# Three of eight row pairs by seven products in the gate-and-up loop, with one weight sum of each on GpSimd

## The reference, cut to what matters

```python
D_MODEL, SEQ = 2048, 256
D_FF = ((8 * D_MODEL // 3 + 255) // 256) * 256      # 5632

def swiglu(x, w_gu, w_down):
    g, u = jnp.split(x @ w_gu, 2, axis=-1)
    return (jax.nn.silu(g) * u) @ w_down

h = h + 0.5 * rmsnorm(swiglu(rmsnorm(h, n_ffn1_pre), w_ffn1_gu, w_ffn1_down), n_ffn1_post)
...
h = h + 0.5 * rmsnorm(swiglu(rmsnorm(h, n_ffn2_pre), w_ffn2_gu, w_ffn2_down), n_ffn2_post)
```

## Time and profile before

| what | value |
|---|---|
| median of three executions | 2454.83 us |
| the profiled execution: time | 2453.54 us |
| the profiled execution: span | 2451.7 us |
| TensorE busy, weight load busy | 2434.3 us, 2019.7 us |
| VectorE busy, ScalarE busy, GpSimd busy | 1662.5 us, 1290.2 us, 439.6 us |
| chunks 1 to 10 of the first layer, of the second | about 57.6 to 479.2 us, 1782.2 to 2203.8 us |

### The profile page before, as it was taken

One profiled execution on the slowest core, in us unless ns is written; L12 is line 12 of the kernel. 1 busy time (PEld: TensorE's weight loads), 2 busy tenths in 40 slices (PEclk: granted clock), 3 DMA queues, 4 the chain that ended last, 5 costly groups with the idle time before them and its releaser, 6 DMA issues.

```text
span 2451.7 us, 31974 instructions
## 1 busy us (share of the span) xinstructions
PE 2434.3 (99%) x11047; PEld 2019.7 (82%) x11047; DVE 1662.5 (68%) x2077; ACT 1290.2 (53%) x1556; POOL 439.6 (18%) x867
## 2 busy tenths in 40 slices
PE   9999999999999999999999999999999999999998
PEld 7888888888888888888888888888888888888887
DVE  6888888855556456677676564465688888885444
ACT  6555555544445456657575444444655555554442
POOL 5212112232012103223142020010112121211000
PEclk9999999999999999999999999999999999999999
DMA  7777777677678765555665676766677677767664
GB/s 242 215 209 215 209 207 220 206 237 217 201 223 263 203 185 161 172 160 160 166 185 164 196 210 194 229 217 191 213 207 221 200 219 206 215 210 252 195 192 145
DMA packets 306061, 498.50 MB, mean 203 GB/s; under 512 B 28461, under 2 KB 102321, under 8 KB 305201
## 3 DMA queue, kind: packets, MB, share of 16 engines
q1 hardware_dynamic: 282336, 457.85, 62.9%
q0 software_dynamic: 23344, 38.95, 5.1%
q10 hardware_dynamic: 288, 0.52, 0.1%
HBM read 471.39 MB, written 8.52 MB: 196 GB/s over the span
## 4 chain that ended last, share of the span: by engine, by line
PE 95%; POOL 1%; DVE 1%; DMA 1%; SPq 1%; issue 1%; ACT 0%; DVEq 0%; POOLq 0%; ACTq 0%
PE acc L727 56%; PE acc L815 30%; PE mix L815 4%; POOL mkh L690 1%; PE acc L770 1%; DMA sq<-mk_scratch 1%; PE acc L752 1%; POOL mkh L687 1%; SPq L396 0%; PE mix L788 0%; SPq L429 0%; PE mix L997 0%; DMA raw<-w_ffn_gu 0%; PE mix L1043 0%; PE mix L1077 0%
## 5 line engine op out<-in xcount | busy, mean ns | idle before, releaser
L1204 ACT ACTIVATE whi<-raw 128x1024 fp32r<-128x1024 f32 x860 | 910.4, 1060 | 1089.7 <-PE acc L727 685.6
L1701 DVE TENSOR_TENSOR wlo<-raw,whi 128x1024 fp32r<-128x1024 f32 x860 | 1044.1, 1225 | 607.5 <-ACT whi L1204 598.5
L815 PE MATMUL acc<-whi,x_lo 128*128 128x512 f32 x1000 | 389.0, 389 | 0.0
L815 PE MATMUL acc<-whi,x_hi 128*128 128x512 f32 x1000 | 389.0, 389 | 0.0
L815 PE MATMUL acc<-wlo,x_hi 128*128 128x512 f32 x1000 | 389.0, 389 | 0.0
L727 PE MATMUL acc<-whi,u_hi 128*128 128x512 f32 x896 | 356.9, 398 | 0.0
L345 POOL DMA_DIRECT2D nat<-nat x416 | 203.4, 497 | 823.9 <-DVE nat L1911 656.7
L727 PE MATMUL acc<-whi,u_lo 128*128 128x512 f32 x896 | 349.4, 390 | 0.0
L727 PE MATMUL acc<-wlo,u_hi 128*128 128x512 f32 x896 | 349.1, 390 | 0.0
L727 PE MATMUL acc<-wlo,act_hi 128*128 128x512 f32 x688 | 267.7, 389 | 0.0
L727 PE MATMUL acc<-whi,act_hi 128*128 128x512 f32 x688 | 267.7, 389 | 0.0
(11 more groups left out here) (423 smaller groups left out, 2928.1 us busy)
## 6 DMA issues: line engine op xcount, KB each, us to landing
raw<-w_ffn_gu SPq DMA_DIRECT2D x352, 512.0 KB
raw<-w_ffn_down SPq DMA_DIRECT2D x176, 512.0 KB
raw<-w_in SPq DMA_DIRECT2D x224, 256.0 KB
raw<-w_in SPq DMA_DIRECT2D x96, 512.0 KB
raw<-w_mem_kv SPq DMA_DIRECT2D x32, 512.0 KB
raw<-w_out SPq DMA_DIRECT2D x32, 512.0 KB
nat<-nat POOLq DMA_DIRECT2D x416, 32.0 KB, 3.9
raw<-w_in SPq DMA_DIRECT2D x64, 128.0 KB
```

The costliest lines, as they stand in the source:

```text
L815: ins = nc.tensor.matmul(bank, sides[a], weights[b], start=start and m == 0, stop=stop and m == 2)
L1204: act(whi[:, l % RING], raw[:, l], ACT.Copy).then_inc(hi_ready, 1)
L1701: tt(wlo[:, l], raw[:, l], whi[:, l % RING].bitcast(fp32), ALU.subtract).then_inc(lo_ready, 1)
```

## The change

`SEVEN_AT` becomes (2, 4, 6): three pairs of eight by seven products. The in-place sum of the up unit goes to GpSimd (`right_sum`); it waits for the second of VectorE's sums, since that one reads what it overwrites. In GpSimd's queue the sum for the first seven stands ahead of the 16 DMAs of the swap, the other two behind them. ScalarE's upper part of the up unit waits for GpSimd's semaphore. VectorE makes the lower parts of the two units of an eight in one operation (`split_pair`), in the odd slot; those of a seven stay single. The combining operations move from slots 12 and 13 to slots 14 and 15. The activation sums of the third seven get room: the side tensors lie elsewhere, `a_sum` in the place of `wsum`, and their split in chunk 0 is made in three pieces one slot later.

```diff
@@ -86,7 +86,7 @@
 SKEW = RING
 QUADS = U_D
 TURN_AT, UPPER_AT, LOWER_AT = 2, 11, 12
-SEVEN_AT = (2, 5)
+SEVEN_AT = (2, 4, 6)
 N7 = len(SEVEN_AT)
 SPLIT_SMALL = 20
 ONCE = {"act_once": ("wsm_hi", "small_T_ready", "small_out", "tanh_b", "lrT_ready", "softplus", "exp_g", "exp_rest"),
...
@@ -287,8 +287,22 @@
         oss = sb("oss", [P, 4])
         gss = sb("gss", [P, NT])
         lr2g = sb("lr2g", [RANK, P])
-        ov = overlay([("junk", [P, CW], mybir.dt.bfloat16)], [("lrT", [RANK, SEQ], fp32)])
+        ov = overlay([("junk", [P, CW], mybir.dt.bfloat16)], [("lrT", [RANK, SEQ], fp32)],
+                     [("last_side_hi", [P, P], f32r), ("last_side_lo", [P, P], f32r)])
         junk, lrT = ov["junk"], ov["lrT"]
+        last_side = ov["last_side_hi"], ov["last_side_lo"]
+
+        def side_tile(s, m):
+
+            n = 3 * s + m
+            return (side_hi[:, n, :], side_lo[:, n, :]) if n < 8 else (last_side[0][:, :], last_side[1][:, :])
+
+        def side_parts():
+
+            two = lambda v: v[:, 0:6, :].rearrange("p (s m) n -> p s m n", m=3)
+            return ((two(side_hi), two(side_lo), side[:, 0:2, 0:3, :]),
+                    (side_hi[:, 6:8, :], side_lo[:, 6:8, :], side[:, 2, 0:2, :]),
+                    (last_side[0][:, :], last_side[1][:, :], side[:, 2, 2, :]))
 
         acc = ctx.enter_context(nc.psum_tensor("acc", [P, 2, NT, CW], fp32))
         mix = ctx.enter_context(nc.psum_tensor("mix", [P, 4, CW], fp32))
...
@@ -585,6 +599,24 @@
                 pl.wait_ge(sem("h_stored"), 4 * b * 16)
                 pl.dma_start(block_res[b][:, :, :], h_v).then_inc(sem("h_in"), 16)
 
+            def right_sum(f, i, s):
+
+                j = 2 * SEVEN_AT[s] + 1
+                n = UB[f"gu{f + 1}"] + i * 2 * U_D + j
+                pl.wait_ge(raw_full[j % RAW], (n // RAW + 1) * LOADED)
+                pl.wait_ge(sem("sums"), sevens(f, i, s, 3, 2))
+                v = raw[:, j % RAW, :, :]
+                pl.tensor_tensor(v[:, 0, :], v[:, 0, :], v[:, 1, :], ALU.add).then_inc(sem("pool_sum"), 1)
+
+            def swaps(f):
+
+                for i in range(1, N_GU):
+                    right_sum(f, i, 0)
+                    swap_act(f * N_GU + i - 1)
+                    for s in range(1, N7):
+                        right_sum(f, i, s)
+                swap_act(f * N_GU + N_GU - 1)
+
             def swap_rows(r, dst, src, before):
 
                 pl.wait_ge(sem("rows_turned"), r + 1)
...
@@ -595,8 +627,7 @@
             rsqrt(R_X)
 
             pl.engine_nop().then_inc(sem("act_lo"), 1)
-            for n in range(N_GU):
-                swap_act(n)
+            swaps(0)
             for c in range(4):
                 if c >= 2:
                     if c == 2:
...
@@ -1311,12 +1341,14 @@
                         for t in range(NT):
                             act(gate_t(t), acc[:, 0, t, :], ACT.Silu,
                                 scale=rs[:, (R_X, R_H2)[f], t:t + 1]).then_inc((sem("gate_row"), acc_out[0])[t], 1)
-                    if j == 13:
+                    if j == 14:
 
                         ac.wait_ge(unit_used, at(n0, i, 2 * U_D, j) + 1)
                         ac.wait_ge(sem("side"), 5 * f + 5)
                         act(seven_rows(x_hi)[:, :, 0, BOTTOM], side[:, :, 3, :], ACT.Copy)
-                        act(side_hi[:, :, :, :], side[:, :, 0:3, :], ACT.Copy).then_inc(sem("side_hi"), 1)
+                        for hi, lo, v in side_parts():
+                            ins = act(hi, v, ACT.Copy)
+                        ins.then_inc(sem("side_hi"), 1)
 
                 slots(n0, i, 2 * U_D, tasks)
 
...
@@ -1329,10 +1361,10 @@
                 for j in range(2 * U_D):
                     s = SEVEN_AT.index((j + LOOK) // 2) if (j + LOOK) // 2 in SEVEN_AT else None
                     if s is not None and j % 2:
-                        ac.wait_ge(sem("sums"), sevens(f, i, s, 4, 3))
+                        ac.wait_ge(sem("pool_sum"), sevens(f, i, s, 1, 1))
                     split(at(n0, i, 2 * U_D, j), (i, n0, 2 * U_D), j)
                     if s is not None and j % 2:
-                        ac.wait_ge(sem("sums"), sevens(f, i, s, 4, 4))
+                        ac.wait_ge(sem("sums"), sevens(f, i, s, 3, 3))
                         act(wsum_hi[:, :, :], wsum[:, :, :], ACT.Copy).then_inc(sem("sum_hi"), 1)
                     if j == UPPER_AT:
                         upper_act(f * N_GU - 1 + i, act_hi[:, ds(i * 4 - 4, 4), :])
...
@@ -1786,13 +1818,14 @@
                         norm_sum(k)
                     if j == 11:
                         sides(f)
-                    if j == 14:
+                    if j == 15:
 
                         ve.wait_ge(sem("side_hi"), f + 1)
                         tt(seven_rows(x_lo)[:, :, 0, BOTTOM], side[:, :, 3, :],
                            seven_rows(x_hi)[:, :, 0, BOTTOM].bitcast(fp32), ALU.subtract)
-                        tt(side_lo[:, :, :, :], side[:, :, 0:3, :], side_hi[:, :, :, :].bitcast(fp32),
-                           ALU.subtract).then_inc(sem("side_lo"), 1)
+                        for hi, lo, v in side_parts():
+                            ins = tt(lo, v, hi.bitcast(fp32), ALU.subtract)
+                        ins.then_inc(sem("side_lo"), 1)
                     if j == 2 * U_D - 1:
                         ve.wait_ge(sem("norm_rs"), norm_at(k))
                         ve.wait_ge(unit_used, at(n0, i, 2 * U_D, j) + 1)
...
@@ -1838,12 +1871,18 @@
                     if s:
                         ve.wait_ge(sem("sum_used"), sevens(f, i, s, 1, 0))
                     tt(wsum[:, 0, :], raw[:, g, 0, :], raw[:, u, 0, :], ALU.add).then_inc(sem("sums"), 1)
-                    ve.wait_ge(sem("sums"), sevens(f, i, s, 4, 1))
+                    ve.wait_ge(sem("sums"), sevens(f, i, s, 3, 1))
                     tt(wsum[:, 1, :], wsum[:, 0, :], raw[:, u, 1, :], ALU.add).then_inc(sem("sums"), 1)
-                    tt(raw[:, u, 0, :], raw[:, u, 0, :], raw[:, u, 1, :], ALU.add).then_inc(sem("sums"), 1)
-                    ve.wait_ge(sem("sums"), sevens(f, i, s, 4, 2))
+                    ve.wait_ge(sem("sums"), sevens(f, i, s, 3, 2))
                     tt(wsum[:, 2, :], wsum[:, 1, :], raw[:, g, 1, :], ALU.add).then_inc(sem("sums"), 1)
-                    ve.wait_ge(sem("sums"), sevens(f, i, s, 4, 4))
+                    ve.wait_ge(sem("sums"), sevens(f, i, s, 3, 3))
+
+                def split_pair(n, j):
+
+                    g = (j + LOOK) % RAW - 1
+                    ve.wait_ge(hi_ready, n + LOOK + 1)
+                    tt(wlo[:, g:g + 2], raw[:, g:g + 2], whi[:, g % RING:g % RING + 2].bitcast(fp32),
+                       ALU.subtract).then_inc(lo_ready, 2)
 
                 def tasks(j):
                     if j == TURN_AT:
...
@@ -1860,18 +1899,20 @@
                         tt(gate_t(1), mix[:, 3, :], up_t(0), ALU.add).then_inc(sem("combined"), 1)
                     if j == 2 * SEVEN_AT[-1] + 3:
                         tt(up_t(0), mix[:, 1, :], up_t(0), ALU.add).then_inc(sem("combined"), 1)
-                        ve.wait_ge(sem("combined"), per_chunk(f, i, 4, 2))
-                        tt(up_t(1), mix[:, 1, :], gate_t(1), ALU.add).then_inc(sem("combined"), 1)
                     if j == 2 * U_D - 2:
                         ve.wait_ge(sem("row_done"), per_chunk(f, i, 2, 1))
                         tt(gate_t(0), acc[:, 0, 0, :], gate_t(0), ALU.add).then_inc(sem("gate_row"), 1)
+                        ve.wait_ge(sem("combined"), per_chunk(f, i, 4, 2))
+                        tt(up_t(1), mix[:, 1, :], gate_t(1), ALU.add).then_inc(sem("combined"), 1)
                         ve.wait_ge(unit_used, at(n0, i, 2 * U_D, j) + 1)
+                        ve.wait_ge(sem("combined"), per_chunk(f, i, 4, 3))
                         tt(gate_t(1), acc[:, 0, 1, :], gate_t(1), ALU.subtract).then_inc(acc_out[0], 1)
                     if j == 2 * U_D - 1:
                         ve.wait_ge(sem("row_done"), per_chunk(f, i, 2, 2))
                         ve.wait_ge(sem("combined"), per_chunk(f, i, 4, 4))
                         tt(up_t(0), acc[:, 1, 0, :], up_t(0), ALU.add).then_inc(sem("up_row"), 1)
                         ve.wait_ge(unit_used, at(n0, i, 2 * U_D, j) + 1)
+                        ve.wait_ge(sem("combined"), per_chunk(f, i, 4, 4))
                         tt(up_t(1), acc[:, 1, 1, :], up_t(1), ALU.add).then_inc(acc_out[1], 1)
 
                 for j in range(2 * U_D):
...
@@ -1879,7 +1920,10 @@
                     s = SEVEN_AT.index((j + LOOK) // 2) if (j + LOOK) // 2 in SEVEN_AT else None
                     if s is not None and j % 2 == 0:
                         weight_sums(j, s)
-                    split(at(n0, i, 2 * U_D, j), j)
+                    if s is not None:
+                        split(at(n0, i, 2 * U_D, j), j)
+                    elif j % 2:
+                        split_pair(at(n0, i, 2 * U_D, j), j)
```

(15 more changed lines are left out.)

## The result

The changed kernel takes **2580.86 us** (median of four runs, 2577.69 to 2582.10), the kernel before, run beside it, 2454.77 (four runs): ratio **1.0511**, 95% interval 1.0498 to 1.0525. The profiled execution has a span of 2576.0 us (2451.7 before).

The account below looks back on a forecast made before the run. TensorE's issue rate bounds the kernel before (42.16 us a chunk); afterwards VectorE's chain, waiting on GpSimd, does. Per layer 0.7 plus nine times 4.43, two layers 81.2 us: forecast 2536 us, range 2492 to 2590.

Parts of the forecast that it names:

- queue and port both hold: Main case: DMA issues block GpSimd's queue and GpSimd excludes VectorE at the SBUF port; 2525 to 2545 us, chance 0.71.
- The queue decides: Second seven's sum waits behind 16 DMA issues; transposes to unit 9's lower part take 11.77 us, VectorE idles 4.94.
- The port: GpSimd's sum holds the shared SBUF port, delaying VectorE's lower part behind the third sum by 0.82 us.
- The sum on GpSimd: Length of the 128x512 in-place sum on GpSimd: 1.20 us, bounds 0.69 and 2.28.
- VectorE's work: VectorE's own operations per chunk after the change: 38.4 us of 41.48, a pair operation taking 2.29.
- VectorE's own chain sets the period: From the second chunk on, VectorE's work plus its waits make each chunk 46.6 us.
- The lead into chunk 1: In chunk 1 VectorE's lead hides most of the delay; TensorE stalls 0.4 us before unit 9, chunk 42.87 us.
- What I cost at nothing: Items priced at zero, among them chunk 0's larger side sums in slots 11 to 15: 2 us a layer if uncovered.
- It does what it says: Rival: issues do not hold GpSimd's queue and the port costs nothing; chunk 41.48 us, 2441 us; faster 0.07.
- Only the port: Rival: queue not held, port is; chunk 42.6 to 43.3 us, 2455 to 2473 us, chance 0.04.
- Only the queue: Rival: DMA issues hold GpSimd's queue, the port costs nothing; 2493 to 2513 us, chance 0.08.
- GpSimd loses every race: Rival: GpSimd gets the port only after the first lower part; chunk 49.8 us, 2599 us; with slow sum 0.10.

Follow-up runs that it names:

- e2: Changed kernel with GpSimd's sum of the second seven put ahead of the 16 DMA issues, the third still behind them: 2488.4 us.
- e4: Changed kernel issuing 4 of the swap's 16 DMAs, the other 12 blocks not exchanged: 2491.5 us.
- e5: Kernel of e1 plus a 128x512 two-input GpSimd operation per seven that nobody waits for: 2481.6 us.
- e6: As e5, with a one-input 128x512 copy on GpSimd in place of the two-input operation: 2464.7 us (one run).
- e1: Changed kernel with the in-place sum of the up unit back on VectorE, all else as changed: 2448.55 us.
- e3: Changed kernel with GpSimd adding only 16 of 512 columns of each sum, queue place and waits kept: 2506.1 us.
- e7: Kernel of e1 with every lower part made in an operation of its own, no pairs: 2449.6 us.
- e10: Kernel of e1 with act_hi and act_lo in slots 7 and 8 instead of 11 and 12: 2452.3 us.
- e9: Kernel of e7 with act_hi and act_lo in slots 7 and 8 instead of 11 and 12: 2453.1 us.

## Why the prediction was right, and where its sizes were off

The direction and the mechanism were right; the size was too small. The time is no proof of the sizes: for the case that came true, queue and port both hold, the prediction gave 2525 to 2545, and 2580.9 is 36 us above that. The full range holds it only because its upper part was drawn for lost races or a slow sum, and neither happened. That part is luck. Two of the signs named for the profile were missed as well: a period of 46 to 47 us, and a first chunk under 43.5.

**The queue decides: right.** The sum starts as the sixteenth issue ends, and 11.94 us (11.77) and 5.07 (4.94) answer to the steps. The test is e2, e4 and the changed kernel: 43.86, 43.87 and 47.8. Out of the queue's way it is 3.9 to 4.0 us a chunk, in e2 and e4 alike; by the prediction's own terms it would be 4.0 (4.94 less 0.82 and 0.15).

**The port: right.** Forecast was 0.82 us lost at each sum. In the changed kernel the lower part behind the third sum takes 2.10 us in place of 1.23, 0.87 more, here in the eighth chunk:

```profile
399.50 2.10 DVE L1733 TENSOR_TENSOR wlo<-raw,whi 128x1024 fp32r<-128x1024 f32 x1
```

Beside an operation that nobody waits for it is 0.84 (e5). The Trainium skill's page "SBUF — State Buffer" (section "SBUF: two separate sides") has it that the shared pair of ports is an exclusive lock, and that the loser blocks for the whole instruction of the other. By e5 and e6 the traces agree: VectorE's sum ends 0.55 us after GpSimd's operation, whichever it is. Of the 2.0 us between e1 and e2, 1.68 answer to e5. The 0.3 left are a net: in e2 GpSimd's sum is waited for, and VectorE has three sums of 0.60 us less to do.

**The sum on GpSimd: 1.20 us, measured 1.30** with VectorE idle, the nearest row's own value; 1.73 where it has to wait 0.43 for VectorE's third sum. The 0.56 us after that sum's start, at which the port was to come free, holds: 303.21 + 0.43 = 303.64, 0.54 after 303.10. The estimate from the Trainium skill's page "GPSIMD Engine Reference" (section 3.1), 1.11, was further off.

**VectorE's work: right in the main.** The pair takes 2.28 us (forecast 2.29). The mechanism of the period is that of the forecast too: in the chunks at full clock VectorE's chain alone sets it, without a wait for TensorE, at 47.27 to 47.32 us.

**Four terms were missing or mis-sized.** The typical chunk is 47.83 us (mean of the second to eighth of the nine distances), forecast 46.6:

1. *VectorE's chain itself is 0.7 us longer than the sum of its terms*, 47.3 and not 46.6. By the starts from 158.85 to 206.13 us: the idling 0.13, the port twice 0.05, the eight operations that combine PSUM with nat 0.19 (5.23, forecast 5.04), the pair ahead of the third seven's sums 0.11 (2.31, forecast 2.20), the rest in steps of a few hundredths. Over nine chunks in two layers this is 12 us.
2. *"VectorE's own chain sets the period"* left TensorE out of the ring. Behind the 2.76 us gap seven or eight matmuls run at half the rate in most chunks; TensorE so uses the second seven's `wsum` later, and VectorE waits for it before the third seven's first sum: the 1.00 us at 327.77. Where the matmuls behind the same gap are not slow, there is no such wait and the chunk takes 47.3 us, so the clock and not the gap is what costs here. In the second layer one chunk has 14 slow matmuls and takes 49.6 us, and some gaps are longer as well. With these, some 13 us in both layers. The ring through `wsum` is there without slow matmuls too, once VectorE's chain is shorter: 0.65 us a chunk in e2, 1.4 in e1.
3. *The lead into chunk 1.* The prediction had the transposes start 9.8 us after the chunk's first matmul, the lower part of unit 9 at 21.6, and a stall of 0.4 us. TensorE's first matmul of the loop starts at 57.47 us (57.41 before), and VectorE's transposes and the lower part of unit 9 here:

```profile
69.78 1.30 DVE L1955 STREAM_TRANSPOSE nat<-nat 128x512 f32<-128x512 f32 x2
81.82 1.23 DVE L1733 TENSOR_TENSOR wlo<-raw,whi 128x1024 fp32r<-128x1024 f32 x1 [4.49 <-ACT whi L1234]
```

   The transposes start 12.3 us in, the lower part of unit 9 at 24.35, and the stall is 2.76 us in chunk 1 already, with slow matmuls behind it. Two things make the 2.5 us. The side work of chunk 0, under *"What I cost at nothing"*, was said to be 2 us a layer if uncovered, and it was: VectorE's first sum starts at 62.22 us, before at 60.25. And the 9.8 takes one sum off VectorE but leaves out the port's loss at the first seven, 0.87, which the same prediction prices elsewhere. The first distance is 48.45 us (43.08 before), so 5.4 and not 0.7 over: with the second layer (5.2) some 9 us more than forecast.
4. *A late burst once a layer*, not foreseen: 51.26 and 51.43 us in place of some 48, 7 us. In the trace of before it is there, hidden by slots of slack. A row read as harmless was so only as long as nobody stood behind GpSimd.

Together 12 + 13 + 9 + 7 = 41 of the 43 us between the forecast 81 and the 124 by which the spans differ.

**The rivals.** *It does what it says* is dead with GpSimd in it, and with VectorE in its place it comes to 2448.6 and not 2441. *Only the port* is e2 and e5: 43.53 to 43.86, above the 42.6 to 43.3 worked out for it; that sum has VectorE's chain 0.7 us short, as above, and leaves out the wait for `wsum` (0.65 us in e2). *Only the queue* is nearest to e3, where GpSimd has the port for 0.23 us: 2506, within the 2493 to 2513 given. *GpSimd loses every race* did not happen: for the first and the third seven it took the port behind the third sum in every group (40 lower parts of 2.1 us); that the wait behind the third sum is what lets it in wasn't tested.

**What e1 still lacks** (41.85 and not 41.48): VectorE waits 1.4 us for the one `wsum`, and what it does behind that comes late for TensorE, the pair behind the transposes in e1 (0.35 us), the release of the last bank in e7 (0.3). Moving act_lo out of that stretch (e10) reaches 41.48, so this is shown to be enough; a second `wsum` wasn't tried.

## What to carry to other kernels

Before giving work to a lightly busy engine, look at what stands in its queue around the slot, not at its busy share: GpSimd was 18% busy, and its queue held the sum up for 4.6 us (314.0 to 318.64) while three engines came to wait for it. Ask who else pays for the place: an operation on GpSimd beside a two-input VectorE operation saved 0.6 us there and cost it 0.84 to 0.87. And when a gap in TensorE is forecast, price the matmuls behind it too, and the buffers that they release late; when a stall is "covered by the lead", check that nothing upstream has eaten the lead.

## What the runs showed of the hardware

- TensorE after an idle gap: behind gaps of 2.04 us (e3, second layer), 2.76 (after) and 3.57 (e9) some matmuls ran at the lower level of the granted clock, 0.43 us apart; behind those of 1.21 (e2) and 1.65 (e3) they did not. The gap alone doesn't decide it: in the changed kernel three gaps of 2.73 to 2.75 us in the first layer (before 179.61, 275.11 and 370.67) have no slow matmul behind them. The Trainium skill's page "TensorE: Matmul & The Clock Gate" (section "Wait — 56ns, not 53.3ns?") gives 426.7 ns from start to start for matmuls of 512 columns at 1.2 GHz, and the trace agrees.
- GpSimd holds up a VectorE operation with two SBUF inputs also when it only copies: by 0.41 us for a copy recorded with 0.94, by 0.84 for an operation with 1.36 (e6, e5). VectorE's operation ended 0.54 to 0.55 us after GpSimd's in both.
- A DMA issue on GpSimd holds it for 0.49 us (16 in 7.8, 4 in 2.0), and the sum behind them starts as the last one ends (318.64).
- GpSimd began one of its bursts per layer late, by 3.1 us in the kernel before and in e10 (1.9 in e2), with no releaser in the trace; the kernel with four issues in place of 16 (e4) showed none.
